# Attention with values as weights and paired outputs, and modulation in four column groups spread over prepare and finish

## The reference, cut to what matters

```python
for l in range(DEPTH):                                   # DEPTH = 2
    mod_l = jnp.split((s_lat @ ada_w[l] + ada_b[l])[:, None, :], 6, axis=-1)   # s = silu(c), ada_w[l]: 1024 x 6144
    mod_c = jnp.split(s_ctx @ ada_w[l] + ada_b[l], 6, axis=-1)
    ...
def attend(q, k, v, map_w):   # diff attention: 2 maps per head, weights (1, -lam); latent attention: 1 map, weight 1
    s = jnp.einsum('bqhmd,bkhmd->bhmqk', q, k).astype(jnp.float32)
    p = jax.nn.softmax(s, axis=-1)
    w = jnp.einsum('bhmqk,mh->bhqk', p, map_w.astype(jnp.float32))
    return jnp.einsum('bhqk,bkhd->bqhd', w.astype(v.dtype), v)
```

## Time and profile before

| | us |
|---|---|
| median of 3 runs | 4515.46 (4511.79 to 4516.79) |
| the profiled execution, its own time | 4513.33 |
| its span in the profile | 4511.4, granted clock 0.92 |
| first modulation (TensorE's first to last record) | 16.1 to 47.9 |
| prepare, layer 0 and 1 | 430.3 to 521.9 and 2860.1 to 2952.3 |
| attention, layer 0: context tiles, latent tiles | 684.6 to 725, 725 to 1105.4 |
| attention, layer 1 (latent tiles only) | 3112.5 to 3485.9 |
| finish, layer 0 (first modulation instruction to the next stage's first matmul) | 1124.9 to 1303.2 |
| finish, layer 1 | 3504.4 to 3562.2 |

### The profile page before, as it was taken

One profiled execution on the slowest core, in us unless ns is written; L12 is line 12 of the kernel. 1 busy time (PEld: TensorE's weight loads), 2 busy tenths in 40 slices (PEclk: granted clock), 3 DMA queues, 4 the chain that ended last, 5 costly groups with the idle time before them and its releaser, 6 DMA issues. The chain is left out here.

```text
span 4511.4 us, 57439 instructions
## 1 busy us (share of the span) xinstructions
PE 3802.8 (84%) x20496; PEld 3071.4 (68%) x20496; DVE 1758.7 (39%) x2503; ACT 1679.3 (37%) x2683; POOL 326.6 (7%) x610
## 2 busy tenths in 40 slices
PE   4997677997987799999998699666998469999997
PEld 1997346776255687787797599444776348877875
DVE  2112754664323432233254411465665443322323
ACT  3113654664433322222243311655665532222222
POOL 0000062110000000000000000044110000000000
PEclk8998786999999899999999899878999689999998
DMA  4123220001732232232255222410000223322323
GB/s 161 58 84 121 95 64 6 7 5 74 292 118 101 84 98 85 87 98 86 86 171 178 102 85 72 154 54 29 7 5 26 70 93 98 94 87 89 94 93 126
DMA packets 128904, 398.45 MB, mean 88 GB/s; under 512 B 17392, under 2 KB 63664, under 8 KB 121136
## 3 DMA queue, kind: packets, MB, share of 16 engines
q1 hardware_dynamic: 105200, 327.21, 22.0%
q0 software_dynamic: 2880, 41.94, 2.3%
q10 hardware_dynamic: 20736, 28.18, 1.8%
HBM read 340.27 MB, written 57.02 MB: 88 GB/s over the span
## 5 line engine op out<-in xcount | busy, mean ns | idle before, releaser
L646 PE MATMUL psum<-part,part 128*128 128x512 f32 (+2 forms) x4240 | 1514.3, 357 | 228.8 <-DVE part L1459 227.8
L647 PE MATMUL psum<-part,part 128*128 128x512 f32 (+2 forms) x4240 | 1508.1, 356 | 0.0
L648 PE MATMUL psum<-part,part 128*128 128x512 f32 (+2 forms) x4240 | 1506.9, 355 | 0.0
L646 PEld LDWEIGHTS psum<-part,part 128*128 128x128 f32 x4240 | 806.9, 190 | 332.0 <-issue 237.0
L1459 DVE TENSOR_TENSOR part<-region,part 128x1024 fp32r<-128x1024 f32 (+4 forms) x446 | 550.5, 1236 | 1154.7 <-ACT part L1363 625.4
L647 PEld LDWEIGHTS psum<-part,part 128*128 128x128 f32 x4240 | 807.3, 190 | 93.7
L648 PEld LDWEIGHTS psum<-part,part 128*128 128x128 f32 x4240 | 806.2, 190 | 94.6
L1363 ACT CAST part<-region 128x1024 fp32r<-128x1024 f32 x220 | 230.6, 1048 | 561.0 <-PE psum L648 511.3
L1763 DVE TENSOR_REDUCE region<-psum 128x1 f32<-128x1280 f32 (+1 forms) x216 | 295.7, 1370 | 262.7 <-PE psum L867 262.4
L893 PE MATMUL psum<-region,region 128*128 128x64 f32 x2624 | 350.7, 273 | 4.2 <-ACT region L1281 4.2
L893 PEld LDWEIGHTS psum<-region,region 128*128 128x128 f32 x2624 | 330.5, 195 | 18.9 <-ACT region L1281 10.1
(11 more groups left out here) (207 smaller groups left out, 3191.0 us busy)
## 6 DMA issues: line engine op xcount, KB each, us to landing
region<-in_ffn_in SPq DMA_DIRECT2D x220, 512.0 KB, 3.5
region<-in_ffn_out SPq DMA_DIRECT2D x80, 704.0 KB, 4.0
region<-in_ada_w POOLq DMA_DIRECT2D x20, 2048.0 KB, 12.9
proj<-region ACTq DMA_DIRECT2D x16, 1720.0 KB, 11.2
region<-proj SPq DMA_DIRECT2D x20, 1376.0 KB, 5.7
region<-in_w_in SPq DMA_DIRECT2D x16, 1376.0 KB, 7.2
region<-proj SPq DMA_DIRECT2D x136, 128.0 KB, 2.3
region<-in_x SPq DMA_DIRECT2D x16, 640.0 KB, 8.0
```

Source lines behind the costliest of these rows:

```text
L646: mm(out, a[0], b[0], start=start, stop=False)
L647: mm(out, a[0], b[1], start=False, stop=False)
L648: return mm(out, a[1], b[0], start=False, stop=stop)
```

## The change

`modulation_rows` uses 32 columns of `sil` (now padded with zeros) as weights, and matmul k writes partitions 32 (k % 4) to 32 (k % 4) + 31, so that four column groups of the array hold two of the eight matmuls each. ScalarE copies all 128 partitions. `modulation_turn` becomes a plain matmul with 128x128 weights and a moving matrix `sel` of two columns, which also adds the four groups up. Finish handles one chunk per tile (10 in all); the other ten chunks are made in prepare, five in each layer, half a chunk per tile, with loads issued by GpSimd in project and prepare. In attention v is the weights (64 columns) and the turned map the moving side (128 columns); the diff output goes to partitions 0 to 63 of bank 7 and the latent one to 64 to 127; ScalarE copies the pair, TensorE turns it back, and VectorE scales it. `VALUE_LAG` goes from 6 to 10 and `PRODUCTS` sets the pieces, which puts value work into slots C and A (12 and 12, then 8 and 8 instructions) and none into B.

```diff
-        A_PT = [take(NT, P) for _ in range(2)]
+        A_PT = [[take(NT, P) for _ in range(2)], [region(R_QKD + (2 + j) * N, NT, P) for j in range(2)]]
+        A_OT = take(P)
...
-        TURN_LAG, VALUE_LAG = 5, 6
+        TURN_LAG, VALUE_LAG = 5, 10
+        KEEP_SLOTS, BACK_SLOTS = 7, 9
         PIECES = ((0, 4), (4, 8), (8, NT))
+        PRODUCTS = ((0, 3), (3, 6), (6, 8), (8, NT), None, None)
...
-            for m in range(VALUE_LAG // 2):
+            for m in range(BACK_SLOTS - 2):
...
-            def modulation_rows(b, w):
+            def modulation_rows(out, w):
+                m = P // ADA_GROUPS
                 for k in range(KD):
-                    last = mm(bank(b, parts=2), sil[:, 2 * k:2 * k + 2], w[:, k, :], start=(k == 0), stop=(k == KD - 1))
+                    g = k % ADA_GROUPS
+                    last = mm(out[g * m:(g + 1) * m, :], sil[:, 2 * k:2 * k + m], w[:, k, :], start=(k < ADA_GROUPS),
+                              stop=(k >= KD - ADA_GROUPS), skip_group_check=True)
...
-                    last = nc.tensor.transpose(bank(b)[:, 2 * m:2 * m + 2], rows[:, m * P:(m + 1) * P], ident[0:2, 0:2])
+                    last = mm(out[:, 2 * m:2 * m + 2], rows[:, m * P:(m + 1) * P], sel[:], start=True, stop=True)
...
@@ prepare, TensorE: multiply @@
+                    if begun(t):
+                        modulation_turn(bank(3)[:, NH * MQ:], P_ROWS, 2)
                     for k in range(2):
                         mm(bank(3, NH * MQ), T_QNT[:, k, :], wuq[:, k, :], start=(k == 0), stop=(k == 1))
...
-                    last.then_inc(sem("made2"), 1)
+                    pe.wait_ge(sem(f"half_in{s}"), 8 * (T - s) + 16)
+                    modulation_rows(bank(5)[:, ADA_HALF:BANK], P_ADA[s]).then_inc(sem("made2"), 1)
...
@@ attention, TensorE @@
-                        for kt in range(*a.pieces[p]):
-                            last = mm(bank(VALUES, HD), A_PT[q % 2][:, kt, :], v[:, kt, h * HD:(h + 1) * HD],
-                                      start=(kt == 0), stop=(kt == a.nk - 1))
+                        for kt in range(first, end):
+                            for w, at in ((1, R_VD), (0, R_VM)):
+                                v = region(at, NT, 256)[:, kt, h * HD:(h + 1) * HD]
+                                last = mm(bank(VALUES, P)[(1 - w) * HD:(2 - w) * HD, :], v, A_PT[h % 2][w][:, kt, :],
+                                          start=(kt == 0), stop=(kt == a.nk - 1), skip_group_check=True)
+                    def turn_back(m, i, h):
+                        pe.wait_ge(sem("ot_kept"), a.heads(i, h) + 1)
+                        at = (3 * (m % 2) + 2) * BANK + 2 * P
+                        nc.tensor.transpose(psum[:, at:at + P], A_OT, ident[:]).then_inc(sem("turned_back"), 1)
...
@@ attention, ScalarE: ahead of a slot's copies, in slot B @@
+                    def keep_values(i, h):
+                        act.wait_ge(sem("pv_made"), a.heads(i, h) + 1)
+                        if begun(a.heads(i, h)):
+                            act.wait_ge(sem("turned_back"), a.heads(i, h))
+                        nc.scalar.copy(A_OT, bank(VALUES, P)).then_inc(sem("ot_kept"), 1)
...
@@ attention, VectorE: ahead of the slot's maximum, in slot A @@
+                        if scores_of is not None:
+                            dve.wait_ge(sem("scored"), a.maps(scores_of, m) + 1)
+                        dve.wait_ge(sem("turned_back"), a.heads(i, h) + 1)
+                        back = (3 * (m % 2) + 2) * BANK + 2 * P
+                        for w in range(2):
+                            at = h * HD if w else (NH + h) * HD
+                            last = v.tensor_scalar(A_OUT[:, a.first + i, at:at + HD],
+                                                   psum[:, back + (1 - w) * HD:back + (2 - w) * HD],
+                                                   A_RL[:, 2 * h + w:2 * h + w + 1], None, ALU.mult)
...
@@ prepare, ScalarE: first in keep_products; VectorE: in keep_queries @@
+                    nc.scalar.copy(P_ROWS, bank(5)[:, ADA_HALF:BANK])
+                        keep_modulation(bank(3)[:, NH * MQ:NH * MQ + 4], ADA_M * prep_chunk[l] + 2 * (t - 1), 2)
...
@@ GpSimd @@
-                            for j in range(ADA_T):
-                                pool.dma_start(F_ADA[s][:, j, :, :].rearrange("p k n -> p (k n)"),
-                                               t["ada_w"][ADA_FIRST // ADA_M + ADA_T * (2 * u + s) + j]
-                                               ).then_inc(sem(f"ada_in{s}"), 16)
+                            pool.dma_start(F_ADA[s].rearrange("p k n -> p (k n)"), t["ada_w"][FIN_CHUNK + 2 * u + s]
+                                           ).then_inc(sem(f"ada_in{s}"), 16)
+            def load_half(l, n):
+                src = t["ada_w"][prep_chunk[l] + n // 2].rearrange("p (k n) -> p k n", k=KD)
+                pool.dma_start(P_ADA[n % 2], src[:, :, n % 2 * ADA_HALF:(n % 2 + 1) * ADA_HALF]
+                               ).then_inc(sem(f"half_in{n % 2}"), 16)
```

More of the change, by code:

```diff
@@ L378, in tile @@
                         joins = (i, m // 3 - 1) if m else (i - 1, NH - 1)
-                    slot(m, i, joins, [before(TURN_LAG, j) for j in range(2)], [before(VALUE_LAG, j) for j in range(2)])
+                    slot(m, i, joins, [half(TURN_LAG, j, 3) for j in range(2)], [half(VALUE_LAG, j, 6) for j in range(2)],
+                         head(KEEP_SLOTS), head(BACK_SLOTS))
             tile(0, True)
@@ L412, in has, with multiplies, last_product @@
                 return at is not None and self.pieces[at[2]] is not None
+            def multiplies(self, at):
+                return at is not None and self.products[at[2]] is not None
+            def last_product(self, p):
+                return p + 1 == sum(x is not None for x in self.products)
         def att_loops(l):
@@ L859, in scores @@
                             pe.wait_ge(sem("exp_done"), a.maps(i, m) - 1)
+                        if a.base and not begun(i) and m == 0:
+                            pe.wait_ge(sem("att_kept"), a.heads(0, 0))
+                        if backs:
+                            turn_back(m, *backs)
                         if r == 0:
@@ L898, in slot, with values @@
-                    def slot(m, i, joins, turns, products):
+                    def values(i, h, p):
+                        first, end = a.products[p]
+                        piece = [j for j, x in enumerate(a.pieces) if x is not None and x[0] < end][-1]
+                        pe.wait_ge(sem("pt_kept"), a.step(i, 2 * h + 1, piece) + 1)
+                        if p == 0 and begun(a.heads(i, h)):
+                            pe.wait_ge(sem("ot_kept"), a.heads(i, h))
+                        for kt in range(first, end):
[3 more added lines that the diff above has]
+                                          start=(kt == 0), stop=(kt == a.nk - 1), skip_group_check=True)
+                        if a.last_product(p):
+                            last.then_inc(sem("pv_made"), 1)
@@ L1449, in first_modulation @@
             def first_modulation():
+                v.tensor_copy(sel[:], ident[:, 0:2])
+                for g in range(1, ADA_GROUPS):
+                    at = g * P // ADA_GROUPS
+                    dve.drain()
+                    v.tensor_tensor(sel[:], sel[:], ident[:, at:at + 2], ALU.add)
+                dve.drain().then_inc(sem("sel_ready"), 1)
                 scan_constants()
@@ L1591, in prepare @@
                 in_steps(dve, NT, [(2, keep_queries), (3, keep_turned), (1, keep_diff), (0, rotate_tile)])
+                dve.wait_ge(sem("half_turned"), l + 1)
+                keep_modulation(bank(3)[:, NH * MQ:NH * MQ + 4], ADA_M * prep_chunk[l] + 2 * (NT - 1), 2)
+                if l == 1:
+                    dve.drain()
+                    for row, gain in ((4, 2), (5, 3)):
+                        with_gain(l, row, gain)
                 handover("dve", dve)
@@ L1792, in slot @@
                             join_maps(*joins)
-                        for at in products:
-                            if a.has(at) and at[2] == a.per - 1:
-                                keep_values(*at[:2])
                     att_tiles(a.count, dve, slot)
@@ L2032, in _ @@
             for l in range(DEPTH):
-                idle()
-                idle()
+                project(l)
+                prepare(l)
                 scan(l)
```

141 lines of the change are left out of this document (83 added, 58 removed).

## The result

The changed kernel takes **4622.68 us** (median of 4 runs, 4615.38 to 4643.61) against 4516.12 before: a ratio of 1.0245, 95% interval 1.0215 to 1.0274. It is slower by 106 us. Forecast were 4517 us and, as the far end of the range, 4556.

What follows compares the result with a forecast made beforehand. The prediction took handovers between engines, not TensorE alone, to bound attention's loop. Attention +58, first finish -82, first modulation -8 and prepare +36 sum to +4 on 4513.3 us: forecast 4517 us, range 4482 to 4556.

Steps and rivals of the forecast that it cites:

- the sum for attention: Attention, both layers: steps added to the head loop outweigh the halved value work, +58 us, bounds +20 and +80.
- The loop of a head: Attention, per head: scalings, turn back, later value work and tiling changes add 0.75 us, a period of 12.2 us.
- The clock in attention: Attention: no term for a change of TensorE's clock, which the profile before showed at 0.97.
- Context heads and emptying loops: Attention: eight context heads cost 0.5 us more each, +4; three loops empty in seven slots instead of three, +6.
- Value instructions: Attention: two column groups run together, 0.056 us per instruction, 2.2 us less TensorE work per head.
- Rival 4: Attention, prepare and finish: the column groups don't overlap, values take 0.107 us each; 4606 us, chance 0.06.
- Rival 1: Attention follows TensorE's work after all, so a head's period falls to 10.2 us; 4380 us, chance 0.07.
- Prepare: Prepare, both layers: added half chunks cost 1.5 us per tile, 18 us per layer, +36 us, bounds +10 and +70.
- First finish: First finish: 9.0 us per tile instead of 16.6 (-68) and an earlier start (-14), together -82 us.
- First modulation: First modulation, at the start: less work after the loads end, -8 us, from -11 to -6.
- Rival 3: Prepare: half loads delay the row's landing and TensorE falls to 1.2 GHz more often; 4551 us, chance 0.22.

Runs made afterwards that it cites:

- e4: The changed kernel with ten useless identity transposes per head added while TensorE waits for the joined maps: 4527.2 us.
- e5: The changed kernel with turn back and VectorE's scalings one slot later, in slot B, and six useless identity transposes per head: 4485.5 us.
- e3: The changed kernel with the value products of a piece reordered, all of one output and then all of the other: 4624.7 us.
- e6: The kernel before with only the modulation part of the change, plus twelve useless identity transposes per prepare tile in a TensorE wait: 4445.2 us.
- e13: The changed kernel with value products in other half-steps, turn back and VectorE's scalings in slot B, no fillers: 4514.1 us.
- e8: The kernel before with every second value product of the latent heads left out and no instruction added: 4552.9 us.

## Why the prediction was wrong

The step that failed is the sum for attention, and in it one assumption that was never written as a term: every handover was priced at 2.4 GHz, because the earlier trace rows showed 0.97. The forecast named the wait that would grow ("the wait of the turn for the join up from 0.6 to about 2 us"; it is 1.36) and asked for the clock in prepare, but not in attention.

- **The loop of a head.** Forecast +0.75 at full clock; e4 gives 12.29 against 11.43, +0.86. Right. Where it comes from was right as well: e5 moves the scalings and the turn back and gets 0.66 of it back.
- **The clock in attention.** Forecast 0; measured 1.37 us per head over a long stretch, and 88 us over both stages (933.0 in after, 844.9 in e4). This is the whole error of the attention term (139 - 58 = 81) and more; what is left, +51, is near the forecast.
- **Context heads and emptying loops.** Forecast +10, measured +13. From the first scores of the context tiles to the first latent scores it is 3.5 us more (701.4 to 751.5, before 684.6 to 731.1), and from the last head's scores to the end of the stage 4.7 and 5.2 us more. The 62 steps from head to head between them took 125 us more.
- **Value instructions.** 0.055 us apart against 0.056 forecast, two column groups at a time. Rival 4 (no overlap) is out. Rival 1 (TensorE's work decides, the reading that the Trainium skill's page TensorEngine Tiling (Array Packing), Performance Considerations, invites) is out too: TensorE's time for the values did halve, and the kernel became slower.
- **Prepare.** Forecast +36, measured +52 in this execution and +34 in that of e3 (109.1 and 109.2), inside the bounds. With the clock held by fillers only +4.1 and +2.5 us are left (e6), against a before at 0.85, so most of what this execution lost here is 1.2 GHz. Whether 1.55 us of added TensorE work, partly hidden, would have been right at one clock, no run shows. The price at 1.2 GHz was in the text as a bound, and should have been the middle, as the stage stood at 0.85 before.
- **First finish.** Forecast -82, measured -61, outside the stated -66 to -92 (by the text's own terms -64 to -93). A tile takes 10.7 instead of 9.0 us, 9 x 1.7 = 15, and the first turn comes 28.4 us after attention, not 23.6. That start was mis-sized: ScalarE takes the first tile's rows up at 1213.1, 19.3 us after attention's end (1193.8), against 22.0 before (1127.4 after 1105.4), so they came 2.7 us sooner; a first turn at 23.6 would have needed them 7.5 us sooner. Less ahead of them in the queues helped less than its share.
- **First modulation.** Forecast -8, measured -6.5, with the turn at 1.2 GHz as the bound had it.

The range ended at 4556. It would have held 4623 only with attention at the lower clock, which no rival had. Rival 3 carried "TensorE, with more waiting, falls to 1.2 GHz more often", for prepare alone; the same sentence about slot B was the missing one. The rows for it were there: slot B was the one place in the head where TensorE stood still, and the change took 2.2 us of work out of that head and put the scalings where they lengthen that stand-still.

## What to carry to other kernels

Taking work off TensorE in a loop that is closed by handovers gains nothing and can cost the clock: before pricing such a change, look for the stretch where TensorE waits, and ask if it gets longer or emptier. Keep steps that feed nobody (a scaling, a turn back) out of the chain that the waiting engine depends on; moving one by a slot was worth 0.66 us a head (e5), and in e13 the same move kept the clock without fillers. Where a wait can't be shortened, a few transposes of a constant into a free bank, ahead of the wait, are a cheap test of whether the clock is the cause, and at times the remedy.

## What the runs showed of the hardware

- In attention of after, with TensorE busy 286 of 341 us and waiting 1.4 us at a time for the joined maps, the granted clock fell from 2.4 to 1.2 GHz for a part of three heads in four; in e13, with 0.6 us for the joined maps and 1.63 us of standing still per head in all, it held 2.4 GHz for 28 heads in a row. The Trainium skill's page TensorE: Matmul & The Clock Gate, in the section on a second failure mode, describes a kernel whose clock swings because TensorE idles briefly between groups of matmuls; these traces agree, 1.36 us idle and a clock of 0.53 in the slot behind it.
- A kernel with less TensorE work can be slower: in e8, with half of the value products left out, a head takes 10.95 us at full clock and 13.0 at 0.74, +36 us in all.
- Transposes of a constant held the clock: with ten of them in the wait of each head (e4) it was 1.00 through 24 heads, where after had 0.84.
- Matmuls of two column groups overlap even when those of one group are listed first and those of the other behind them, fully in pieces of two matmuls each (eight instructions in 0.66 us in either order), only in part in pieces of three (e3: twelve in 1.15 us, paired 0.88).
